# Late up-units of an expert layer as products of 512 columns, their low halves on GpSimd, one-hot rows from an index row in PSUM

## The reference

```python
def peer_ffn(h, w_q, sub_keys, u_tab, v_tab):
    q = (h @ w_q).reshape(b, s, PEER_HEADS, 2, PEER_HALF)
    sc = jnp.einsum('bshpc,hpkc->bshpk', q, sub_keys).astype(jnp.float32)
    top_v, top_i = lax.top_k(sc, PEER_TOPK)
    ...                                   # 16 best of the pairs, idx = i1 * 128 + i2
    gate = jax.nn.softmax(best_v, axis=-1)
    def expert_chunk(args):
        u = u_tab[ix]
        act = jax.nn.gelu(jnp.einsum('chkd,cd->chk', u, hx).astype(jnp.float32))
        vv = v_tab[ix]
        return jnp.einsum('chk,chkd->cd', (gx * act).astype(vv.dtype), vv)
```

## Time and profile before

| | us |
|---|---|
| median of 3 runs | 1877.04 |
| lowest, highest | 1873.39, 1878.48 |
| profiled execution, span | 1874.2 |
| PE busy | 1824.1 (97%) |
| DVE busy | 1305.0 (70%) |
| ACT busy | 922.9 (49%) |
| POOL busy | 116.3 (6%) |
| late part (first `spread` to last up-unit) | 478.2 to 783.3 |

### The profile page before, as it was taken

The page is one execution under the profiler, slowest core; times in us unless marked ns, Lnnn a source line. Parts: engine busy times, 40 slices in busy tenths (PEclk is TensorE's granted clock), DMA queues, the critical chain, the costliest instruction groups (busy, mean ns, idle before and its releaser), DMA issues.

```text
span 1874.2 us, 30697 instructions
## 1 busy us (share of the span) xinstructions
PE 1824.1 (97%) x12639; PEld 1677.6 (90%) x12639; DVE 1305.0 (70%) x2098; ACT 922.9 (49%) x1238; POOL 116.3 (6%) x75
## 2 busy tenths in 40 slices
PE   7999899999999999999999999999999999989998
PEld 7999899999999999988888888888888889878887
DVE  5567875999788888755555557887577445757744
ACT  6447635444344343444444445766455343546533
POOL 0000002670000000000000000030000000100000
PEclk9999999999999999999999999997999999989999
DMA  6444345454444443465555553421155456625543
GB/s 236 162 159 161 132 180 204 168 188 170 153 155 147 146 158 137 160 232 193 189 200 186 195 197 124 148 83 64 65 183 179 178 200 221 175 96 206 186 169 145
DMA packets 44757, 310.66 MB, mean 166 GB/s; under 512 B 5182, under 2 KB 5694, under 8 KB 8160
## 3 DMA queue, kind: packets, MB, share of 16 engines
q1 hardware_dynamic: 42592, 303.58, 44.9%
q0 software_dynamic: 1472, 4.86, 1.4%
q10 hardware_dynamic: 576, 0.55, 0.1%
HBM read 306.84 MB, written 2.13 MB: 165 GB/s over the span
## 4 chain that ended last, share of the span: by engine, by line
PE 69%; DVE 12%; ACT 2%; issue 1%; POOL 0%; ACTq 0%; DVEq 0%
PE bank L347 20%; PE bank L1706 18%; PE bank L3034 9%; PE bank L358 6%; PE bank L362 3%; PE bank L1677 3%; PE bank L3293 2%; DVE s_arena L1846 1%; DVE s_ring_lo L310 1%; PE bank L446 1%; PE bank L2659 1%; DVE s_arena L1843 1%; DVE s_arena L1889 1%; DVE s_arena L2121 1%; PE bank L2597 1%
## 5 line engine op out<-in xcount | busy, mean ns | idle before, releaser
L310 DVE TENSOR_TENSOR s_ring_lo<-s_ring,s_w_hi 128x2048 fp32r<-128x2048 f32 x227 | 519.7, 2290 | 173.1 <-ACT s_w_hi L304 168.6
L304 ACT ACTIVATE s_w_hi<-s_ring 128x2048 fp32r<-128x2048 f32 x244 | 465.8, 1909 | 132.1 <-PE bank L347 42.3
L347 PE MATMUL bank<-s_h_r,s_w_hi 128*128 128x256 f32 x3072 | 405.2, 285 | 0.3 <-DVE s_arena L3522 0.3
L347 PEld LDWEIGHTS bank<-s_h_r,s_w_hi 128*128 128x128 f32 x3072 | 381.7, 192 | 4.8 <-issue 3.6
L1706 PE MATMUL bank<-s_w_hi,s_h_r 128*128 128x512 f32 x1008 | 238.8, 389 | 0.3 <-issue 0.3
L1706 PEld LDWEIGHTS bank<-s_w_hi,s_h_r 128*128 128x128 f32 x1008 | 189.2, 188 | 39.6 <-issue 0.4
L347 PE MATMUL bank<-s_h_r,s_ring_lo 128*128 128x256 f32 x1536 | 215.7, 283 | 1.4 <-DVE s_ring_lo L310 1.4
L347 PEld LDWEIGHTS bank<-s_h_r,s_ring_lo 128*128 128x128 f32 x1536 | 198.1, 192 | 1.8 <-DVE s_ring_lo L310 1.8
L1806 ACT ACTIVATE s_h_r<-s_arena 128x512 fp32r (+1 forms) x64 | 40.4, 632 | 184.6 <-PE bank L1706 184.6
L3006 DVE TENSOR_TENSOR s_ring_lo<-s_ring,s_spare_r 128x2048 fp32r<-128x2048 f32 x32 | 73.1, 2291 | 78.6 <-ACT s_spare_r L2992 78.6
L1706 PE MATMUL bank<-s_ring_lo,s_h_r 128*128 128x512 f32 x504 | 124.5, 389 | 0.0
(11 more groups left out here) (464 smaller groups left out, 2501.3 us busy)
## 6 DMA issues: line engine op xcount, KB each, us to landing
s_ring<-weights SPq DMA_DIRECT2D x282, 1024.0 KB, 4.8
s_arena<-bias_by_distance POOLq DMA_DIRECT2D x12, 384.0 KB, 7.9
s_arena<-mem SPq DMA_DIRECT2D x1, 1024.0 KB, 5.7
s_x<-x SPq DMA_DIRECT2D x1, 1024.0 KB, 13.4
x_away<-s_x SPq DMA_DIRECT2D x1, 1024.0 KB, 7.9
s_arena<-sub_keys SPq DMA_DIRECT2D x1, 1024.0 KB, 11.0
s_arena<-x_away SPq DMA_DIRECT2D x1, 1024.0 KB, 8.4
out<-s_x SPq DMA_DIRECT2D x2, 512.0 KB, 2.6
```

What stands on the lines that cost most here:

```text
L304: act.activation(k.w_hi[:, u % 2, :], k.ring[:, u % RING, :], ACT.Copy).then_inc(k.hi_ready, 1)
L310: dve.tensor_tensor(k.ring_lo[:, u % RING, :], k.ring[:, u % RING, :], plain(k.w_hi[:, u % 2, :]), ALU.subtract).then_inc(k.lo_ready, 1)
L347: last = pe.matmul(out[:, nb * S:(nb + 1) * S], w[:, c, nb * P:(nb + 1) * P], h[:, c, :], start=(n == 0 and c == 0), stop=(n == 2 and c == 7))
```

## The change

- Late up-units run through a new `unit_T_banks`: half `nb` has a bank of its own, `ps[nb]`, and gets 8 matmuls of 512 columns (high weights with low and high input side by side, `h_swapped`) and 8 of 256 (low weights with high input, added to the second 256 columns). `half_done` is counted after the first half.
- `cross(j)` on ScalarE, last in the turn of unit j, copies columns 0 to 255 of each half's bank to one buffer `across` in SBUF; `join(j)` on VectorE, also last in the turn, adds it to columns 256 to 511 and writes half a bank of `ps[2 + j % 2]`. Gelu and combination work there. TensorE's half waits for the join of the same half of the unit before (`summed`), no longer for a combination or gelu two units back.
- The groups go round three banks, `ps[4]` to `ps[6]`, in place of six. `ps[7]` holds a copy of the index row, from which `heat` reads.
- The low halves of units 22 to 63 and of the first down-unit go to GpSimd.
- On VectorE `heat(g + 1)` now comes first in a turn, ahead of combination and multiplication.
- Semaphores are shared or renamed (`dve_prepared`, `act_prepared`), and `gdn_small` becomes a part of the new tile `joined`.

```diff
--- before.py
+++ after.py
@@ -346,6 +346,25 @@
             for c in range(8):
                 last = pe.matmul(out[:, nb * S:(nb + 1) * S], w[:, c, nb * P:(nb + 1) * P], h[:, c, :],
                                  start=(n == 0 and c == 0), stop=(n == 2 and c == 7))
+    last.then_inc(k.unit_done, 1)
+
+
+def unit_T_banks(k, pe, u, h_hi, h_swapped, banks, half_done, free):
+
+
+    hi, lo = unit_parts(k, u)
+    split_ready(k, pe, u, 0)
+    for nb in range(2):
+        free(nb)
+        for c in range(8):
+            pe.matmul(banks[nb][:, :], hi[:, c, nb * P:(nb + 1) * P], h_swapped[:, :, c, :], start=(c == 0), stop=False)
+        if nb == 0:
+            split_ready(k, pe, u, 2)
+        for c in range(8):
+            last = pe.matmul(banks[nb][:, S:2 * S], lo[:, c, nb * P:(nb + 1) * P], h_hi[:, c, :],
+                             start=False, stop=(c == 7))
+        if nb == 0:
+            last.then_inc(half_done, 1)
     last.then_inc(k.unit_done, 1)
 
 
...
@@ -1608,7 +1627,12 @@
         return F + j
 
     up_at = up_turns()
-    bank = [ps[2 + g % 6] for g in range(GROUPS)]
+    bank = [ps[4 + g % 3] for g in range(GROUPS)]
+    iota = ps[7][:, 0:KEYS]
+    H_SPLIT, SHIFTED = 1, 2
+    QUERY_SPREAD, EXPS = 1, 2
+    across = k.joined[:, :]
+    h_swapped = k.h_r[:, 0:2]
 
     def present(g):
 
...
@@ -1663,16 +1687,24 @@
 
             if j < 2:
                 pe.wait_ge(q_out, PEER_H)
-            elif j - 2 < EARLY_R:
+            elif j < EARLY_R:
                 pe.wait_ge(gelu_out, j - 1)
-            else:
-                pe.wait_ge(combined, j - 1 - EARLY_R)
-            unit_T_split(k, pe, split_unit(j), *h_pair, ps[j % 2])
+            if j < EARLY_R:
+                unit_T_split(k, pe, split_unit(j), *h_pair, ps[j % 2])
+                return
+
+            def free(nb):
+                if j == EARLY_R:
+                    pe.wait_ge(gelu_out, EARLY_R - 1 + nb)
+                else:
+                    pe.wait_ge(summed, 2 * (j - 1 - EARLY_R) + nb + 1)
+
+            unit_T_banks(k, pe, split_unit(j), k.hT_hi, h_swapped, ps[0:2], half_done, free)
 
         def spread(g):
             pe.wait_ge(hot_ready, g + 1)
-            if g >= 6:
-                pe.wait_ge(spread_out, g - 5)
+            if g >= 3:
+                pe.wait_ge(spread_out, g - 2)
             for n in range(GROUP_T):
                 last = pe.matmul(bank[g][:, n * KEYS:(n + 1) * KEYS], hot[:, g % 2, 0, n, :],
                                  hot[:, g % 2, 1, n, :], start=True, stop=True)
...
@@ -1771,9 +1803,13 @@
         def gelu(j):
 
 
-            act.wait_ge(k.unit_done, F + j + 1)
-            out = flat(k.G[:, 2 * j:2 * j + 2, :]) if j < EARLY_R else ps[j % 2][:, :]
-            act.activation(out, ps[j % 2][:, :], ACT.Gelu_apprx_tanh).then_inc(gelu_out, 1)
+            if j < EARLY_R:
+                act.wait_ge(k.unit_done, F + j + 1)
+                act.activation(flat(k.G[:, 2 * j:2 * j + 2, :]), ps[j % 2][:, :], ACT.Gelu_apprx_tanh)\
+                   .then_inc(gelu_out, 1)
+                return
+            act.wait_ge(summed, 2 * (j - EARLY_R + 1))
+            act.activation(ps[2 + j % 2][:, :], ps[2 + j % 2][:, :], ACT.Gelu_apprx_tanh).then_inc(gelu_out, 1)
 
         def copy(g):
 
...
@@ -1784,10 +1820,22 @@
                            bank[g][:, :].rearrange("p (t n) -> p n t", t=GROUP_T)[:, c:, :], ACT.Copy)\
                .then_inc(spread_out, 1)
 
+        def cross(j):
+
+
+            for nb in range(2):
+                if nb == 0:
+                    act.wait_ge(half_done, j - EARLY_R + 1)
+                else:
+                    act.wait_ge(k.unit_done, F + j + 1)
+                if j > EARLY_R or nb:
+                    act.wait_ge(summed, 2 * (j - EARLY_R) + nb)
+                act.activation(across, ps[nb][:, 0:S], ACT.Copy).then_inc(crossed, 1)
+
         for j in range(EARLY_R):
             if j == EARLY_R - 4:
-                act.wait_ge(shift_ready, 1)
-                act.activation(shifted, shifted, ACT.Exp).then_inc(exp_ready, 1)
+                act.wait_ge(dve_prepared, SHIFTED)
+                act.activation(shifted, shifted, ACT.Exp).then_inc(act_prepared, 1)
             gelu(j)
             split_hi(k, act, split_unit(j + 2))
         act.wait_ge(chosen_turned, 1)
...
@@ -1801,6 +1849,8 @@
                     split_hi(k, act, split_unit(j + 1))
             if g >= 1:
                 copy(g - 1)
+            if g in up_at:
+                cross(up_at[g])
         act.wait_ge(multiplied, GROUPS)
         act.wait_ge(spread_mm, GROUPS)
         round_up = lambda d, at: act.activation(weighted_hi[:, d % 2], k.G[:, at, :], ACT.Copy)\
...
@@ -1827,7 +1877,7 @@
                 seam.squares(act, dh, tt)
 
     def gpsimd(pool):
-        for u in range(Q + 2, F + POOL_R):
+        for u in (*range(Q + 2, F + POOL_R), *range(F + EARLY_R + 2, F + PAIRS + 1)):
             n = u - k.whole_units
             pool.wait_ge(k.hi_ready, n + 1)
             pool.wait_ge(k.lo_ready, n)
...
@@ -1955,10 +2005,10 @@
                 dve.wait_ge(spread_mm, g - 1)
             for n in range(GROUP_T):
                 i1, gate = (slotsT[:, c, g * GROUP_T + n:g * GROUP_T + n + 1] for c in (0, 2))
-                dve.tensor_scalar(hot[:, g % 2, 0, n, :], k.iota, i1, gate, ALU.is_equal, ALU.mult)
+                dve.tensor_scalar(hot[:, g % 2, 0, n, :], iota, i1, gate, ALU.is_equal, ALU.mult)
             i2 = slotsT[:, 1, g * GROUP_T:(g + 1) * GROUP_T].rearrange("p (t n) -> p t n", n=1)\
                 .to_broadcast([P, GROUP_T, KEYS])
-            dve.tensor_tensor(hot[:, g % 2, 1, :, :], over(k.iota, GROUP_T), i2, ALU.is_equal)\
+            dve.tensor_tensor(hot[:, g % 2, 1, :, :], over(iota, GROUP_T), i2, ALU.is_equal)\
                .then_inc(hot_ready, 1)
 
         def multiply(g):
...
@@ -1977,7 +2027,7 @@
 
             t = g * GROUP_T
             dve.wait_ge(gelu_out, j + 1)
-            act, at = halves(ps[j % 2][:, :]), k.G[:, 2 * j:2 * j + 2, :]
+            act, at = halves(ps[2 + j % 2][:, :]), k.G[:, 2 * j:2 * j + 2, :]
             if t:
                 dve.wait_ge(spread_out, g)
                 last = dve.tensor_tensor(at[:, :, 0:t], at[:, :, 0:t], act[:, :, 0:t], ALU.mult)
...
@@ -1985,17 +2035,28 @@
                 last = dve.tensor_copy(at[:, :, t:], act[:, :, t:])
             last.then_inc(combined, 1)
 
+        def join(j):
+
+
+            for nb in range(2):
+                dve.wait_ge(crossed, 2 * (j - EARLY_R) + nb + 1)
+                dve.tensor_tensor(ps[2 + j % 2][:, nb * S:(nb + 1) * S], ps[nb][:, S:2 * S], across,
+                                  ALU.add).then_inc(summed, 1)
+
+        own.up(dve.tensor_copy(iota, k.iota))
+        own.settle(dve)
         dve.wait_ge(slots_ready, 2)
         dve.wait_ge(k.unit_done, F)
         heat(0)
         for g in range(GROUPS + 1):
+            if g + 1 < GROUPS:
+                heat(g + 1)
             if g in up_at and up_at[g] > EARLY_R:
                 combine(up_at[g] - 1, max(g - 1, 0))
-                split_lo(k, dve, split_unit(up_at[g] + 1))
             if g >= 1:
                 multiply(g - 1)
-            if g + 1 < GROUPS:
-                heat(g + 1)
+            if g in up_at:
+                join(up_at[g])
         take = lambda d, at: dve.tensor_tensor(weighted_lo[:, d % 2], k.G[:, at, :], plain(weighted_hi[:, d % 2]),
                                                ALU.subtract).then_inc(weighted_ready, 1)
         dve.wait_ge(weighted_round, 1)
...
@@ -2007,6 +2068,8 @@
                 return
             dve.wait_ge(weighted_round, i * 4 + (d + 2))
             take(d + 1, bass.ds(i * 8 + 2 * (d + 1), 2))
+            if d == 0:
+                dve.wait_ge(k.lo_ready, F + PAIRS + 1 - k.whole_units)
             split_lo(k, dve, split_unit(PAIRS + d + 1), turn=i * 4)
 
         downs(dve, body)
...
@@ -3680,7 +3743,8 @@
         k.cols = sb("cols", [P, NCOLS])
         k.rows = sb("rows", [P, NROWS])
         k.small = sb("small", [P, 64])
-        k.gdn_small = sb("gdn_small", [P, 7, 4, GDN_H])
+        k.joined = sb("joined", [P, S])
+        k.gdn_small = k.joined[:, 0:7 * 4 * GDN_H].rearrange("p (a b c) -> p a b c", a=7, b=4)
         k.half_b = sb("half_b", [P, 48])
         k.rate = sb("rate", [P, 2 * LRU_B])
         k.slots = sb("slots", [P, 3, S])
```

More of the change, by code:

```diff
@@ L1595, in peer @@
     x_back = carve(k, 0, TT, D)
-    names = ("keys_here", "q_out", "score_mm", "score_out", "shift_ready", "exp_ready",
-             "chosen_ready", "chosen_turned", "slots_ready", "h_split", "gelu_out", "hot_ready", "spread_mm",
+    names = ("keys_here", "q_out", "score_mm", "score_out", "dve_prepared", "act_prepared", "half_done", "crossed", "summed",
+             "chosen_ready", "chosen_turned", "slots_ready", "gelu_out", "hot_ready", "spread_mm",
              "multiplied", "spread_out", "combined", "weighted_round", "weighted_ready", "bank_done",
```

(18 more changed lines are left out.)

## The result

| | before | after |
|---|---|---|
| median, us | 1875.28 (4 runs, 1873.39 to 1878.48) | 1887.42 (4 runs, 1886.96 to 1888.62) |
| ratio | | 1.006, 95% interval 1.0046 to 1.0075 |
| span of the profiled execution, us | 1874.2 | 1885.1 |
| late part: first late up-unit to first down-unit | 472.2 to 783.3 | 472.7 to 798.2 |

What follows compares the result with a forecast made beforehand. The late expert stage was taken as bound by TensorE's instruction stream. Products -7.5, late low halves +21, end +1.5 and start +0.4 gave +15.4 us on 1874.2; with the median's offset and rounding 1893 us, range 1880 to 1905.

Steps and rivals of the forecast that it cites:

- Products: TensorE's late up-units: wide matmuls make a unit 5.58 us instead of 5.75, saving 7.5 us over 44 units.
- Selects with the index row in PSUM: VectorE's one-hot rows: 401 ns per select instead of 342, so 1.86 us of rows per group instead of 1.62.
- The chain behind two groups: Late stage, rows through ScalarE to GpSimd's low half: ready at about 11.0 us, wanted by TensorE at 9.99.
- the price of one wait: TensorE waiting for GpSimd's low half: 1.0 us lost at each of 21 gaps of two groups, 21 us.
- The start: Start of the late stage, VectorE and ScalarE beginning with full queues: 0.4 us once.
- The end: Ahead of the first down-unit, factors queue behind the last copy and join: TensorE idle 2.0 us instead of 0.45, cost 1.5.
- Sum: All terms together: +15.4 us on the profiled span of 1874.2 us, 1893 us as median.
- it all fits: Rival: low-half chain shorter than 9.99 us, TensorE never waits; -5.6 us, 1871 us; chance 0.17.
- The copy buffer: Rival: late units' copy and join through one buffer bind, 11 us more, 1904 us; chance 0.08.
- held off by GpSimd: Rival: late-stage VectorE work waits while GpSimd runs, 19.8 us a pair, +120 us, about 1997; chance 0.03.

Runs made afterwards that it cites:

- narrow products: Against the kernel with rows after the copy, each group of 8 matmuls of 512 columns made as 16 of 256 into the same bank; 1880.2 us (one run).
- rows after the copy: Against the changed kernel, VectorE makes group g+1's one-hot rows after combination and multiplication again, still ahead of the joins; 1870.58 us, ratio to before 0.9962.
- gelu first: Against the changed kernel, ScalarE does gelu and rounding in the turn after the unit, ahead of that turn's copy; one-hot rows stay first; 1874.8 us (one run).

## Why the prediction was right, and where its sizes were off

The forecast was 1893 us (1880 to 1905), the time 1887.4; by late part (first late up-unit to first down-unit) +15.4 us were forecast and +14.4 measured. The mechanism is the one forecast. That the sum is so near is in part luck, since two wrong sizes offset each other. Point by point:

- **Products**, 5.58 us a unit: 5.59 measured, and the narrow products show that 512 columns are what saves it. Right. (5.59 is from the kernel with the rows after the copy, which has no waits inside a unit.)
- **Selects with the index row in PSUM**, 401 ns from a surcharge on another row: 403 ns. The rows took 664.80 to 666.68 = 1.88 us in the timeline of the kernel after, 1.86 forecast. These are the groups of instructions, 478 to 800 us:

```profile
L2008 DVE TENSOR_SCALAR s_hT<-bank,s_slots 128x128 f32<-128x128 f32 x255 | 86.9, 403 | 1.0
...
L2043 DVE TENSOR_TENSOR bank<-bank,s_joined 128x256 f32<-128x256 f32 x88 | 38.1, 432 | 93.6 <-ACT s_joined L1833 93.6
L1833 ACT ACTIVATE s_joined<-bank 128x256 f32<-128x256 f32 x87 | 33.3, 382 | 70.7 <-PE bank L364 54.5 <-DVE bank L2043 15.7
```

- **The chain behind two groups**, forecast from a unit's last issue: rows at 1.21, multiplication 3.07, gelu 3.83, rounding 4.34, GpSimd 6.32, TensorE 11.0. In the timeline of the kernel after, counted from 678.31:

```profile
678.31 1.88 PEld L1709 LDWEIGHTS bank<-s_hT 128*128 128x128 f32 x16
...
679.52 1.37 DVE L2008 TENSOR_SCALAR s_hT<-bank,s_slots 128x128 f32<-128x128 f32 x4
...
681.40 0.54 DVE L2022 TENSOR_TENSOR s_arena<-s_arena,bank 128x376 f32<-128x376 f32 x1
...
682.15 0.59 ACT L1812 ACTIVATE bank<-bank 128x512 f32<-128x512 f32 x1
682.67 1.90 ACT L304 ACTIVATE s_w_hi<-s_ring 128x2048 fp32r<-128x2048 f32 x1
...
684.65 4.61 POOL L1884 TENSOR_TENSOR s_ring_lo<-s_ring,s_w_hi 128x2048 fp32r<-128x2048 f32 x1 [5.15 <-ACT s_w_hi L304]
...
689.32 0.77 PEld L364 LDWEIGHTS bank<-s_h_r,s_ring_lo 128*128 128x128 f32 x6 [1.04 <-POOL s_ring_lo L1884]
```

That is 1.21, 3.09, 3.84, 4.36, 6.34, 11.01, and 21 waits as counted. **Mis-sized, the price of one wait**: 1.0 us was taken as lost whole, but TensorE gets 0.12 back. The eight narrow products after a wait are issued in 0.94 us (674.57 to 675.51) instead of 1.06. So 21 x 0.88 = 18.5 us, not 21.
- **The start**, 0.4 us forecast. In the timeline of the kernel after:

```profile
479.37 0.97 PEld L1709 LDWEIGHTS bank<-s_hT 128*128 128x128 f32 x8 [0.98 <-DVE s_hT L2011]
...
481.64 1.69 PEld L360 LDWEIGHTS bank<-s_h_r,s_w_hi 128*128 128x128 f32 x8 [1.30 <-issue]
```

0.98 us for the first rows (0.25 before) and 1.30 for the first join: 2.0 us. **Mis-sized**: the index row's own copy and the dearer selects stand in front of the first rows, and the join stands behind the rows of group 1, which I had named but not added up. The 0.4 us had no row behind them.
- **The end**, 2.0 us of idle instead of 0.45: 1.94. Right:

```profile
798.21 3.48 PEld L1738 LDWEIGHTS bank<-s_w_hi,s_h_r 128*128 128x128 f32 x16 [1.94 <-issue]
```

- **Sum**: -7.5 + 18.5 + 2.0 + 1.5 = 14.5 us, and 14.4 are there. The time is 5.6 us below the forecast, and the late part explains 1.0 of them. 4.0 are the part behind it, 1086.9 us in this trace and 1090.9 in that of before, with the granted clocks told above; the forecast took it as unmoved and didn't foresee them. The remaining 0.6 is what is left of three smaller items: the forecast was rounded up by 0.6, the median of after lies 2.3 us above the profiled span where 2.8 was taken, and what stands ahead of the late part is 0.5 longer.
- **Rivals.** That it all fits was what the kernels with the rows after the copy and with gelu first made of it, with 1.9 us taken out of the chain. Its 1871 us agrees with 1870.6 by luck: of its 5.6 us below before the late part shows 1.5, because the gaps at both ends and a stretch of lower clock behind the first of them took the rest. The copy buffer didn't bind in the changed kernel, but it was closer than the 0.5 to 1.2 us that I took as left, which no row showed. In every second unit the join ends some 0.3 to 0.5 us ahead of the wide products that wait for it, at 671.44 against 671.87 in the timeline of the kernel after:

```profile
671.01 0.43 DVE L2043 TENSOR_TENSOR bank<-bank,s_joined 128x256 f32<-128x256 f32 x1 [0.63 <-ACT s_joined L1833]
...
671.87 1.69 PEld L360 LDWEIGHTS bank<-s_h_r,s_w_hi 128*128 128x128 f32 x8
```

As soon as VectorE had the low halves back, TensorE did wait there, 2.4 us on average. VectorE was not held off by GpSimd in the late part, because of the index row in PSUM; without it the late part is 61 us longer than in the changed kernel.

## What to carry to other kernels

Where one engine is the bound and others only owe it something, write down for each debt the chain from its first releaser in queue order, with every instruction that stands ahead of a link on its engine, and compare it with the time at which it is wanted: here 11.0 against 10.0 us decided, while over the whole program VectorE was 67% busy, ScalarE 51% and GpSimd 17%. Moving work to a slower engine is paid in that chain, not in the engine's share; an operation that waits for a late partner should stand behind, not ahead of, the one that starts such a chain. And before work goes to GpSimd beside a busy VectorE, look where VectorE's operations of that stretch read: here moving one index row from SBUF to PSUM was worth 59 us in one order and 114 in the other.

## What the runs showed of the hardware that I had not expected

Selects of 128 elements that read SBUF, 340 ns at the median, took up to 4683 ns beside GpSimd, and two GpSimd operations 0.47 us apart held a group of four for 7.15 us in all; the cost for the kernel was 59 us. A comparison with two SBUF inputs that began just behind a GpSimd operation lengthened that operation by 0.65 to 0.7 us instead. With a TensorE gap of 2.3 us ahead of the first down-unit the granted clock fell to its lower level for some time (0.60 as the mean of 784 to 786 us with the rows after the copy) in all three traces with that gap, while gaps of 2.17 us (narrow products), 1.94 (the changed kernel) and 0.45 (before) left it at 1.00; behind the gaps at the start of the late part it fell in one trace (0.91 from 480 to 500 us, with the rows after the copy) and not in two others with the same gaps (the changed kernel, gelu first). Behind the first down-unit, where no edit changes the work, traces differed by 6.7 us, and the granted clock with them.
